# Branch products of the gates' stage in three fp32r parts, and the residual loaded by chunk

## The reference, cut to what matters

```
xn     = RMSNorm(x);  gA = xn @ w_gA;  gB = xn @ w_gB          # 1024 -> 1024 each
merged = sigmoid(gA) * (o_a @ w_pa) + sigmoid(gB) * (o_b @ w_pb)
h      = x + merged @ w_o
h      = h + cross_attn(RMSNorm(h), mem) ...
```

## Time and profile before

| | |
|---|---|
| median of 3 runs | 2256.56 us |
| lowest and highest run | 2249.81, 2257.85 us |
| the profiled execution's own time | 2258.33 us |
| its span, first to last instruction | 2256.6 us |
| mean granted TensorE clock, share of full speed | 0.956 |
| TensorE busy, VectorE busy, ScalarE busy | 92%, 52%, 28% of the span |

### The profile page before, as it was taken

How to read it: one execution, slowest core, us unless ns; L and a number is a source line. 1 busy time by engine, 2 the same in 40 slices (tenths; PEclk the granted TensorE clock), 3 DMA queues, 4 the chain that set the end, 5 groups by cost and what they waited for, 6 DMA issues and landing times. The chain is left out here.

```text
span 2256.6 us, 39646 instructions
## 1 busy us (share of the span) xinstructions
PE 2072.3 (92%) x16992; PEld 1731.0 (77%) x16992; DVE 1172.6 (52%) x1560; ACT 634.3 (28%) x1220; POOL 149.7 (7%) x209
## 2 busy tenths in 40 slices
PE   8999967789899789978999999777999999999998
PEld 7999954565465555548898898665888889999998
DVE  5222243655688778962222335667655554444445
ACT  4000004440444233321111223354334332122111
POOL 0000000001460011110000000000000000000000
PEclk9999977879899999999999999899999999999999
DMA  6113132020697589964111130300333235223311
GB/s 206 47 46 131 38 114 85 2 62 6 221 334 286 210 298 352 354 222 171 38 51 40 54 122 10 112 20 29 122 103 97 100 128 190 84 84 103 103 29 76
DMA packets 171995, 275.19 MB, mean 122 GB/s; under 512 B 28491, under 2 KB 150323, under 8 KB 166500
## 3 DMA queue, kind: packets, MB, share of 16 engines
q1 hardware_dynamic: 156664, 155.80, 22.2%
q0 software_dynamic: 15120, 117.51, 14.2%
q10 hardware_dynamic: 92, 0.20, 0.0%
HBM read 233.98 MB, written 83.50 MB: 141 GB/s over the span
## 5 line engine op out<-in xcount | busy, mean ns | idle before, releaser
L2023 DVE TENSOR_TENSOR hT<-hT,ps 128x1032 f32<-128x1032 f32 x64 | 78.7, 1229 | 206.3 <-PE ps L1789 206.3
L1789 PE MATMUL ps<-xn_hi,mlp_w 128*128 128x344 f32 x1152 | 181.7, 319 | 0.0
L1789 PEld LDWEIGHTS ps<-xn_hi,mlp_w 128*128 128x128 f32 x1152 | 181.4, 189 | 0.2
L1789 PE MATMUL ps<-mlp_u,mlp_w 128*128 128x344 f32 x1152 | 181.3, 319 | 0.0
L1789 PEld LDWEIGHTS ps<-mlp_u,mlp_w 128*128 128x128 f32 x1152 | 180.8, 188 | 0.0
L1288 PE MATMUL ps<-mla_rt,q_now 32*32 32x256 f32 x4608 | 143.4, 382 | 13.5 <-issue 6.8
L1381 DVE STREAM_TRANSPOSE mla_rt<-qkvT 128x1536 f32<-128x1536 f32 x72 | 124.4, 1758 | 27.9 <-DMA qkvT<-in_cache_mla,page_rows 22.6
L2925 PE MATMUL ps<-xn_hi,gate_w_hi 128*128 128x344 f32 x576 | 128.0, 331 | 7.2 <-DVE gates L2480 3.1
L1288 PEld LDWEIGHTS ps<-mla_rt,q_now 32*32 32x32 f32 x4608 | 84.8, 105 | 57.1 <-issue 31.6
L2925 PE MATMUL ps<-xn_hi,win_hi 128*128 128x344 f32 x576 | 123.8, 323 | 3.5 <-DVE xn_lo L3189 3.5
L2925 PE MATMUL ps<-gates_xn_lo,gate_w_hi 128*128 128x344 f32 x576 | 123.3, 322 | 0.0
(11 more groups left out here) (461 smaller groups left out, 3532.5 us busy)
## 6 DMA issues: line engine op xcount, KB each, us to landing
out_s_dsa_w<-in_cache_dsa_w SPq DMA_DIRECT2D x8, 4094.0 KB, 81.1
u_scr<-mlp_z POOLq DMA_DIRECT2D x32, 512.0 KB, 3.1
mlp_u_raw<-u_scr POOLq DMA_DIRECT2D x32, 512.0 KB, 3.9
obT<-in_w_in SPq DMA_DIRECT2D x23, 512.0 KB
gate_w<-in_w_in SPq DMA_DIRECT2D x16, 512.0 KB, 4.0
oaT<-in_w_up SPq DMA_DIRECT2D x8, 1024.0 KB, 5.9
obT<-in_w_up SPq DMA_DIRECT2D x8, 1024.0 KB, 6.4
oaT<-in_w_down SPq DMA_DIRECT2D x32, 256.0 KB, 2.9
```

The lines of the kernel that those rows point to most:

```text
L1789: last = nc.tensor.matmul(ps[:, NT * (d % 2) + t, 0:TC], wring[:, i % WS, w, k, :], x[:, k, t * TC:(t + 1) * TC], start=(k == 0 and n == 0 ...
L2023: nc.vector.tensor_tensor(h, h, ps[:, NT * (d % 2):NT * (d % 2) + NT, 0:TC], ALU.add).then_inc(drained, 1)
```

## The change

From step 1 on the branch products go in three fp32r parts as the gate products do: 18 matmuls instead of 6 for j = 0, 36 instead of 12 for j = 1. The branch products of step 0 stay in float32. ScalarE makes the upper parts of the branch weights, VectorE the lower parts, in every step from 1 on (`branch_upper`, `branch_lower`). In step 1 they also split `oaT` (2 chunks) and `obT` (4 chunks) once: the upper parts go to the space of `hT` (`oh`), the lower parts overwrite `oaT` and `obT` themselves (`ol`); the split weights also lie in the space of `hT`. ScalarE waits for `merged` = 2 ahead of that. Since the space of `hT` is in use until the last branch product, GpSimd loads `hT` behind that product, in 8 chunks with a semaphore each, and `sums(c)` waits for its own chunk. Step 1 is written out on TensorE, ScalarE, VectorE and SyncE, and the loop runs over steps 2 to 6 or 7. In the loop SyncE loads the branch weights as soon as the split of those before is done, no longer behind the branch product.

```diff
-    h_in = sem("h_in")
+    h_in = [sem(f"h_in{k}") for k in range(KD)]
...
+            oh = place("branch_x_hi", [P, 6, T], -KD * T * 4, F32R)
+            wph = place("branch_w_hi", [P, 2, 4, P], 6 * T * 4 - KD * T * 4, F32R)
+            wpl = place("branch_w_lo", [P, 2, 4, P], 6 * T * 4 + 8 * P * 4 - KD * T * 4, F32R)
+            KC, FIRST = (2, 4), (0, 2)
+            xb = [oaT[:, 0], oaT[:, 1]] + [obT[:, k] for k in range(4)]
+            ol = place("branch_x_lo", [P, 6, T], -(KD + 6) * T * 4, F32R)
...
 # SyncE
-                            if not isinstance(i, int):
-                                sp.wait_ge(prod, i * 2 + (j - 1))
+                            if isinstance(i, int):
+                                at_least(sp, prod, i * 2 + (j - 1) if i else 0)
+                            else:
+                                sp.wait_ge(wp_lo[j], i - 1)
                             sp.dma_start(wp[:, j, 0:kc], w[:, :, at(i * P, P)]).then_inc(w_in_p[j], 16)
                             at_least(sp, lo_made[j], i)
                             sp.dma_start(raw[:, j], w_in[:, :, at(i * P + off, P)]).then_inc(landed[j], 16)
...
 # GpSimd
-                    pool.wait_ge(merged, 2)
-                    pool.dma_start(hT[:], x_scr).then_inc(h_in, 16)
-                    pool.wait_ge(h_in, 16)
+                    pool.wait_ge(prod, 2 * KD)
+                    for k in range(KD):
+                        pool.dma_start(hT[:, k], x_scr[:, k]).then_inc(h_in[k], 16)
+                    for k in range(KD):
+                        pool.wait_ge(h_in[k], 16)
...
 # TensorE
+                    def split_product(i, j):
+                        pe.wait_ge(wp_lo[j], i)
+                        pe.wait_ge(prod_read, i * 2 + j)
+                        if isinstance(i, int) and i == 1:
+                            pe.wait_ge(xb_lo, FIRST[j] + KC[j])
+                        for k in range(KC[j]):
+                            n = FIRST[j] + k
+                            for m, (w, x) in enumerate(((wph, oh[:, n]), (wph, ol[:, n]), (wpl, oh[:, n]))):
+                                for t in range(NT):
+                                    last = nc.tensor.matmul(ps[:, 3 + t, 0:TC], w[:, j, k, :], x[:, t * TC:(t + 1) * TC],
+                                                            start=(k == 0 and m == 0), stop=(k == KC[j] - 1 and m == 2))
+                        last.then_inc(prod, 1)
...
 # ScalarE
+                    def branch_upper(i, j):
+                        if isinstance(i, int) and i == 0:
+                            return
+                        act.wait_ge(w_in_p[j], i * 16 + 16)
+                        act.wait_ge(prod, i * 2 + (j - 1))
+                        if isinstance(i, int):
+                            act.wait_ge(merged, 2)
+                            for n in range(FIRST[j], FIRST[j] + KC[j]):
+                                nc.scalar.activation(oh[:, n], xb[n], ACT.Copy).then_inc(xb_hi, 1)
+                        nc.scalar.activation(wph[:, j, 0:KC[j]], wp[:, j, 0:KC[j]], ACT.Copy).then_inc(wp_hi[j], 1)
+
                     def step(i):
                         upper(i, 0)
-                        if isinstance(i, int):
+                        branch_upper(i, 0)
+                        if isinstance(i, int) and i == 0:
                             mm_weigh(act)
                         else:
                             sigmoid(1, i * 2)
                         upper(i, 1)
+                        branch_upper(i, 1)
                         sigmoid(0, i * 2 + 1)
...
 # VectorE
                     def sums(c):
                         s = c % 2
+                        dve.wait_ge(h_in[c], 16)
                         dve.wait_ge(made[s], c // 2 + 1)
...
+                    def branch_lower(i, j):
+                        if isinstance(i, int) and i == 0:
+                            return
+                        if isinstance(i, int):
+                            for n in range(FIRST[j], FIRST[j] + KC[j]):
+                                dve.wait_ge(xb_hi, n + 1)
+                                nc.vector.tensor_tensor(ol[:, n], xb[n], oh[:, n].bitcast(F32),
+                                                        ALU.subtract).then_inc(xb_lo, 1)
+                        dve.wait_ge(wp_hi[j], i)
+                        nc.vector.tensor_tensor(wpl[:, j, 0:KC[j]], wp[:, j, 0:KC[j]], wph[:, j, 0:KC[j]].bitcast(F32),
+                                                ALU.subtract).then_inc(wp_lo[j], 1)
+
                     def step(i):
...
                         lower(i, 0)
+                        branch_lower(i, 0)
...
                         lower(i, 1)
+                        branch_lower(i, 1)
...
-                    dve.wait_ge(h_in, 16)
```

More of the change, by code:

```diff
@@ L2186, in stage_rest @@
             wp = sb(st, "branch_w", [P, 2, 4, P])
+            oh = place("branch_x_hi", [P, 6, T], -KD * T * 4, F32R)
[4 more added lines that the diff above has]
+            ol = place("branch_x_lo", [P, 6, T], -(KD + 6) * T * 4, F32R)
+            wp_hi, wp_lo = ([sem(f"branch_{x}{j}") for j in range(2)] for x in ("w_hi", "w_lo"))
+            xb_hi, xb_lo = sem("branch_x_hi"), sem("branch_x_lo")
             sg = sb(st, "gates", [P, 2, T])
@@ L2240, in _ @@
                     sp.dma_start(rstd[:], rstd_scr).then_inc(rstd_in, 16)
-                    with sp.Fori(1, KD) as i:
+                    step(1)
+                    with sp.Fori(2, KD) as i:
                         step(i)
@@ L2285, in gate_product @@
                         last.then_inc(gate, 1)
-                    def branch_product(i, j):
-                        at_least(pe, w_in_p[j], i * 16 + 16)
-                        at_least(pe, prod_read, i * 2 + j)
+                    def split_product(i, j):
[10 more added lines that the diff above has]
+                        last.then_inc(prod, 1)
+                    def branch_product(i, j):
+                        if not (isinstance(i, int) and i == 0):
+                            split_product(i, j)
+                            return
+                        pe.wait_ge(w_in_p[j], 16)
+                        at_least(pe, prod_read, j)
                         src, kc = (oaT, 2) if j == 0 else (obT, 4)
@@ L2311, in _ @@
                     step(0)
-                    with pe.Fori(1, KD - 1) as i:
+                    step(1)
+                    with pe.Fori(2, KD - 1) as i:
                         step(i)
@@ L2376, in upper @@
                         if j == 0:
-                            at_least(act, gate, i * 2 - 1 if not isinstance(i, int) else 0)
+                            at_least(act, gate, i * 2 - 1)
                         else:
@@ L2394, in step @@
                         upper(i, 1)
+                        branch_upper(i, 1)
                         sigmoid(0, i * 2 + 1)
-                    steps(act, KD, step)
+                    step(0)
+                    step(1)
+                    with act.Fori(2, KD) as i:
+                        step(i)
                     def wo_upper(c):
@@ L2493, in _ @@
                     link = Link(dve, mm_own)
+                    def branch_lower(i, j):
+                        if isinstance(i, int) and i == 0:
+                            return
+                        if isinstance(i, int):
[6 more added lines that the diff above has]
+                                                ALU.subtract).then_inc(wp_lo[j], 1)
                     def step(i):
-                        if isinstance(i, int):
+                        first = isinstance(i, int) and i == 0
+                        if first:
                             mm_new(dve, link)
                         lower(i, 0)
-                        if isinstance(i, int):
+                        branch_lower(i, 0)
+                        if first:
                             mm_weights(dve, link)
@@ L2509, in step @@
                         gated(i, 0, i * 2 + 1)
-                        if isinstance(i, int):
+                        if first:
                             mm_out(dve)
-                    steps(dve, KD, step)
+                    step(0)
+                    step(1)
+                    with dve.Fori(2, KD) as i:
+                        step(i)
                     wo_lower(0)
```

## The result

| | before | after |
|---|---|---|
| median of 7 runs each | 2257.85 us | 2242.55 us |
| lowest and highest run | 2249.81, 2268.51 us | 2234.43, 2247.6 us |
| ratio after / before, 95% interval | | 0.9929 [0.9912, 0.9946] |
| the profiled execution, its span | 2258.33, 2256.6 us | 2247.6, 2245.6 us |
| from the first matmul of the gate product (1, 0) to the first of the product with w_o | 233.59 us | 220.42 us |

The changed kernel is faster by 0.7%, 16 us by the ratio, between 12 and 20 by its interval. The last row of the table, "the stage" from here on, is 1064.05 to 1297.64 before and 1063.21 to 1283.63 after: 13.17 us less, where 13.2 were forecast. The profiled execution after is the slowest of its seven.

A forecast was written before the change was run, and what follows sets the result against it. TensorE's summed instructions were taken to bound the stage. Seven steps at 1.89 us gave 13.2 us, all else costed at nothing: 2258.33 - 13.2 = 2245.1 us profiled, 2243.3 us against the median; range 2238 to 2251.

The forecast's parts named there:

- What bounds the stage: Steps 1 to 7 of the gates' stage: TensorE's instructions set the time, busy 232.26 of 233.00 us.
- The price of a matmul and the sum: Branch products: fp32r matmul 0.1576 us, float32 0.557; 1.89 us gained a step, 13.2 us over seven steps.
- rival 1, first half: Behind each branch product 0.26 us stays, being from the change of product; gain 9.6 us; chance 0.25 including a step 1 stall.
- rival 2: Branch products: three parts take 3/4 of a float32 product's time; gain 17.3 us, 2239 us; chance 0.05.
- Step 1: The only tight place: splits of `oaT` and `obT` ahead of `gated`; cost taken as 0, bounds 0 and 4.4 us.
- So nothing is lost, by 0.3 us: Step 1: `gated(1, 0)` done at 1078.2, ahead of TensorE's need at 1078.5 us, with gate weights split 4.0 us after issue.
- the bound of 4.4: Step 1: if the gate weights' load still took 8.7 us, TensorE would stand for 4.4 us.
- `hT` late is hidden: Load of `hT` moved behind branch product (7, 1): even 14 us for chunk 0 is hidden, cost nothing.
- the margin given: Product with w_o: a late chunk 0 of `hT` holds up TensorE only at chunk 2, another 11 us on.
- Rivals 3 and 4: 3: late branch weights stall each step, 2281 us, chance 0.05; 4: lower clock behind the stage, about 2256 us, 0.10.

The follow-up runs named there:

- runs of one branch: Changed kernel with only the j = 1 or only the j = 0 branch products split, the other in float32: stage 224.69 and 229.00 us.
- two-part run: Changed kernel without the third part of each branch product (lower weights times upper x): stage 201.23 us.
- the change again: The changed kernel itself, unaltered, timed a second time beside the kernel before: 2241.34 us, ratio 0.9939 [0.9917, 0.9962].

## Why the prediction was right

- **What bounds the stage**: right. TensorE is busy all but 1.5 us of it before and after.
- **The price of a matmul and the sum**: the sum is right, and so is the fp32r price. 1.92 us a step (33.11 to 31.19) for 1.89, 13.17 in all for 13.2, and each branch by itself 8.90 and 4.59 for 8.8 and 4.4. The float32 price of 0.557 was too low, it is 0.578. It did no harm because the gains were counted from the start of a product to the end of the gate triple behind it, where the missing part lay.
- **The open 0.26 us behind each product** (rival 1, first half): it goes with the type. It is there behind float32 products only, in the change and in the runs of one branch, and by the reading above it is the end of the last float32 matmul.
- **Three quarters** (rival 2): the Trainium skill (FP8 and Floating Point Precision, TensorE Precision Notes) has true float32 in 4 passes; by the estimate of three quarters from it the stage would have got 17 us shorter. The trace disagrees: the part matmul is 0.157 us by the two-part run, three of them 82% of a float32 one of 0.578. The 85% of the prediction came from the 0.557.
- **Step 1**: the place was right and its margin wrong by half a microsecond. "So nothing is lost, by 0.3 us" failed at the step that took 4.0 us from issue to split; it was 5.0, with 0.3 us won back on the chain behind the split (8.8 for 9.1) and 0.15 by an earlier issue, and 0.23 us were lost. The size was also not one number: the same code lost 0 to 0.7 in four runs. With `hT` beside it the loss is 4.1 by the rule, for the bound of 4.4.
- **`hT` late is hidden**: right, and the load moved alone costs nothing. But the margin given was wrong: a late chunk 0 is felt not 11 us after chunk 0 of the product but 6.7, since the square and two splits follow its sum.
- **Rivals 3 and 4**: no idle row in any loop step. The spell of lower clock behind the stage does vary (0.79 from 1440 to 1500 us before, 0.74 from 1426 to 1486 after): from the first w_o matmul to the end the runs with that part unchanged take 957 to 962 us, among them before 958.96, after 961.97 and the change again 958.48. That is spread, not a loss by the change.

The whole came out at 2242.55 us for 2243.3. That closeness is partly luck, as the runs of either kernel spread over 13 to 19 us, where the range had counted on 8; the stage is where the forecast can be held to its number.

## What to carry to other kernels

Price a split product from a stretch that consists of the same matmuls, and a float32 product by the spacing of its own records, since the start of the next product can be written before its last matmul is through; a gain of half a per cent is then read off the stage in one trace, while in the whole time it drowns in the scatter of other stages. When operands are split on the fly, put in each queue first what waits for nothing or for the smaller load: work that stands behind a load takes over the load's lateness.

## What was not expected of the hardware

- A small load from SyncE's queue got through no sooner than a large one from GpSimd's that was issued at nearly the same time: 512 KB of gate weights were split 5.0 us after their issue alone, and 13.0 us after it (1065.99 to 1079.02) beside 3612 KB, which themselves landed in 11.5 us.
- After 8 us of idle time TensorE came back at a granted clock of 0.50 and stayed there about 3.2 us, which cost another 1.5 us.
- The same code ahead of the stage differed by 10 us between two executions; some 6 of them arose in one stretch of 95 us, at a granted clock of 0.69 in the one and 0.82 in the other.
